# Two stages with no end inside: the delta heads, and the ssd part of a kernel on one core

## The reference

```python
qkv = jax.nn.silu(centred_dwconv(p[..., :DN_CONV_DIM], conv_w))
t_inv = triangular_solve(eye + a, eye)          # a: beta k k^T decay, strictly lower
v_new = u_i - w_i @ s
o = qd_i @ s + qk_i @ v_new                      # one chunk of the scan
s = s * gl_i + kd_i^T @ v_new
y = (rms_norm(o) * silu(z)) @ w_out
```

```python
xbc = jax.nn.silu(centred_depthwise_conv(xbc, conv_w, conv_b))   # x, B, C: 12 tiles
dt = jax.nn.softplus(dt_raw + dt_bias)
y = ssd_chunked(xs, dt, a, bm, cm)               # 16 heads, forward and backward
y = (y_f + y_b + xs * d_skip) * silu(z)          # z: 8 tiles
```

## Time and profile before

| what | us |
|---|---|
| median of three runs (2258.82 to 2260.98) | 2260.4 |
| the profiled execution | 2255.24 |
| its span, first to last instruction | 2253.5 |
| TensorE busy in it | 1979.7 (88%) |
| VectorE busy in it | 1049.9 (47%) |
| delta heads, from the first a_t transpose to the stage's end | 159.7 to 965.7 |
| ssd part, first product to the next part's first | 1293.9 to 1519.8 |

### The profile page before, as it was taken

The page is one execution under the profiler, slowest core; times in us unless marked ns, Lnnn a source line. Parts: engine busy times, 40 slices in busy tenths (PEclk is TensorE's granted clock), DMA queues, the critical chain, the costliest instruction groups (busy, mean ns, idle before and its releaser), DMA issues. The chain is left out here.

```text
span 2253.5 us, 40621 instructions
## 1 busy us (share of the span) xinstructions
PE 1979.7 (88%) x16700; PEld 1460.5 (65%) x16700; DVE 1049.9 (47%) x2118; ACT 587.4 (26%) x1255; POOL 76.1 (3%) x50
## 2 busy tenths in 40 slices
PE   5889898989898898789788787888899899989998
PEld 2356666666666566544376676666777598878887
DVE  3355756575656657511115417777544554221101
ACT  1033433434343434300103203223333322000000
POOL 0000101011010101000000000000000000000000
PEclk9899999999899999989899888998999999999999
DMA  8710101010101010022131232123000321434443
GB/s 333 298 52 7 57 2 59 1 58 1 59 1 58 8 51 1 2 112 75 42 113 38 78 140 89 65 89 132 31 30 30 140 76 44 165 132 156 157 170 131
DMA packets 52242, 184.77 MB, mean 82 GB/s; under 512 B 5856, under 2 KB 9312, under 8 KB 51552
## 3 DMA queue, kind: packets, MB, share of 16 engines
q1 hardware_dynamic: 52064, 182.23, 21.9%
HBM read 180.11 MB, written 2.10 MB: 81 GB/s over the span
## 5 line engine op out<-in xcount | busy, mean ns | idle before, releaser
L780 PE MATMUL banks<-u,w_ring 128*128 128x512 f32 x768 | 355.5, 600 | 6.5 <-PEq L195 6.5
L410 PE MATMUL banks<-u,w_ring 128*128 128x256 f32 x1088 | 248.8, 391 | 14.8 <-PEq L195 14.8
L410 PEld LDWEIGHTS banks<-u,w_ring 128*128 128x128 f32 x1088 | 212.4, 197 | 48.7 <-issue 18.9
L780 PEld LDWEIGHTS banks<-u,w_ring 128*128 128x128 f32 x768 | 141.1, 192 | 136.6 <-issue 133.4
L3146 PE MATMUL banks<-gated,w_ring 128*128 128x512 f32 (+1 forms) x384 | 140.7, 529 | 2.8 <-PEq L195 2.8
L386 PE MATMUL banks<-u,w_ring 128*128 128x256 f32 x480 | 118.8, 400 | 5.4 <-PEq L225 5.4
L441 PE MATMUL banks<-u,w_ring 128*128 128x256 f32 (+1 forms) x384 | 102.1, 430 | 20.2 <-PEq L195 20.2
L3146 PEld LDWEIGHTS banks<-gated,w_ring 128*128 128x128 f32 x384 | 73.9, 193 | 69.3 <-issue 66.0
L386 PEld LDWEIGHTS banks<-u,w_ring 128*128 128x128 f32 x480 | 94.0, 203 | 20.1 <-issue 7.6
L441 PEld LDWEIGHTS banks<-u,w_ring 128*128 128x128 f32 x384 | 75.4, 197 | 46.9 <-issue 38.0
L807 DVE SCALAR_TENSOR_TENSOR acc<-raw,hc,acc 128x512 f32<-128x512 f32 x128 | 96.2, 752 | 4.6
(11 more groups left out here) (496 smaller groups left out, 3227.1 us busy)
## 6 DMA issues: line engine op xcount, KB each, us to landing
w_ring<-in_w SPq DMA_DIRECT2D x321, 512.0 KB, 6.0
h<-in_h SPq DMA_DIRECT2D x2, 2048.0 KB, 9.6
const_base<-in_const SPq DMA_DIRECT2D x1, 1216.0 KB, 5.4
hold<-h SPq DMA_DIRECT2D x1, 1024.0 KB, 5.8
const_part<-in_const SPq DMA_DIRECT2D x1, 1024.0 KB, 4.8
h<-hold SPq DMA_DIRECT2D x1, 1024.0 KB, 9.2
out<-u SPq DMA_DIRECT2D x8, 128.0 KB, 1.9
const_part<-in_const SPq DMA_DIRECT2D x1, 640.0 KB, 4.4
```

The source lines that it names most:

```text
L410: last = nc.tensor.matmul(out, lhs[k], rhs[k], start=(k == 0), stop=(k == n - 1))
L780: mm = nc.tensor.matmul(self.places[m % len(self.places)][:, :], st.slot(m)[:, P * k:P * k + P], u[:, k, :], start=(k == 0), stop=(k == KT ...
```

## The change

Delta: the seven loop bodies and the last one become one stage, written out head after head, with every semaphore counted on from head to head (`COUNTS`, `due`, `up`). The loads go through `in_stage`. Waits that the stage's end gave for free are now written: `chained`, `dec_ready`, `o_out`, `gate_in`, `raw_out`, `kq_norm`, `silu` at the start of a head. `SCAN` goes down by one product in seven gaps, and the sixth tile (the second gate) of head n+1's front is projected in head n+1, four products ahead of the a_t transposes and four behind them. The output's transposes move before rows 2 and 3, and VectorE's output multiplications between its chains.

Ssd: all ten stages become one. The 36 projected tiles (12 of x, B, C, 8 of z, 16 of rwkv) run in one order on TensorE, in groups of six chunks; each x, B or C tile is taken out, convolved and turned behind its projection; the steps are made beside them; then 16 heads, with the decay rows two heads ahead. ScalarE makes the middle tap of the convolution with the bias; the silu is one VectorE operation. B and C are projected first, so the weights are laid out anew.

```diff
-    LAST, SCAN, REST = 1, ((0, 4, 4), (4, 4, 3), (4, 4, 3), (4, 4, 0)), 2
+    LAST, SCAN, REST = 1, ((0, 3, 3), (3, 3, 3), (3, 3, 3), (4, 3, 0)), 2
...
+        with stage(nc, names + front_names) as (s, block):
+            fronts = [Front(s, zs_of[(n + 1) % 2], hs_of[(n + 1) % 2], n) for n in range(QK_HEADS - 1)]
+            st.in_stage(QK_HEADS - 1, DN_GROUP, s["proj"], block)
...
+                if made:
+                    made.products(pe, KT // 2)
+                for c in (0, 2, 1, 3):
+                    if made:
+                        pe.wait_ge(s["chained"], made.up("chained", c + 1))
+                        pe.wait_ge(s["dec_ready"], made.up("dec_ready", 3 + c // 2 if c < 3 else 4))
+                        pe.wait_ge(s["o_out"], 2 * n)
+                    for t in range(TT):
+                        mm = nc.tensor.transpose(tile(bank[2 * (c % 2) + c // 2], t), tile(a_t[:, c, :], t), C("ident"))
+                    mm.then_inc(s["a_done"], 1)
+                if made:
+                    made.products(pe, KT // 2)
+                    pe.wait_ge(s["raw_out"], made.up("raw_out", 4))
+                    pe.wait_ge(s["kq_norm"], made.up("kq_norm", 2))
...
+                if more:
+                    front.scaled(dve, link)
+                    front.conv(dve, link, 3)
+                    front.chain(dve, link, 0)
+                    output(0)
+                    front.chain(dve, link, 1)
+                    output(1)
+                    front.chain(dve, link, 2)
+                    front.chain(dve, link, 3)
+                    front.silu(dve, link, 3)
```

The TensorE order of the ssd stage, and VectorE's heads:

```diff
+            extra.products(pe, 2 * KT)
+            step_rows()
+            extra.products(pe, 3 * KT)
+            step_sums()
+            for j in range(1, 8):
+                extra.products(pe, KT)
+                if j == 3:
+                    scores()
+                if j >= behind:
+                    turn(j - behind)
+            for j in range(8 - behind, 8):
+                extra.products(pe, KT)
+                turn(j)
+            rows(0)
+            rows(1)
+            for hh in range(SSM_HEADS):
+                if hh + 2 < SSM_HEADS:
+                    rows(hh + 2)
+                extra.products(pe, share(hh) // 2)
+                products(hh)
+                extra.products(pe, share(hh) - share(hh) // 2)
...
+            for hh in range(SSM_HEADS):
+                weights(hh)
+                if hh + 2 < SSM_HEADS:
+                    gaps(hh + 2)
+                if hh % 2 == 0 and hh:
+                    finished(hh // 2 - 1)
```

More of the change, by code:

```diff
@@ new lines, in scores, with turn @@
+            def scores():
+                pe.wait_ge(s["silu"], 4)
+                for g in range(2):
+                    for t in range(ST):
+                        mm = nc.tensor.matmul(bank[g][:, SEQ * t:SEQ * t + SEQ], p[:, 16 + g, P * t:P * t + P], p[:, 18 + g, :],
+                                              start=True, stop=True)
+                    mm.then_inc(s["cb_done"], 1)
+            def turn(j):
+                pe.wait_ge(s["silu"], 5 + j)
+                if j >= 2:
+                    pe.wait_ge(s["turned_out"], j - 1)
+                for t in range(ST):
+                    mm = nc.tensor.transpose(bank[2 + j % 2][:, P * t:P * t + P], p[:, 8 + j, P * t:P * t + P], C("ident"))
+                mm.then_inc(s["turned"], 1)
@@ new lines, in rows @@
+            def rows(hh):
+                if hh == 0:
+                    pe.wait_ge(s["steps"], 4)
+                    pe.wait_ge(s["cb_out"], 4)
+                if hh == 1:
+                    pe.wait_ge(s["turned_out"], 8)
+                if hh >= 2:
+                    pe.wait_ge(s["gaps"], 2 * hh - 2)
+                for d in range(2):
+                    for t in range(ST):
+                        mm = nc.tensor.matmul(bank[2 * (hh % 2) + d][:, P * t:P * t + P], col(hh, S_AC, d, t).to_broadcast([P, P]),
+                                              C("ident"), start=True, stop=True)
+                    mm.then_inc(s["rows"], 1)
@@ new lines, in products @@
+            def products(hh):
+                pe.wait_ge(s["weights"], hh + 1)
+                j, at = hh // 2, 64 * (hh % 2)
+                if j >= 2 and hh % 2 == 0:
+                    pe.wait_ge(s["done"], j - 1)
+                for t in range(ST):
+                    mm = nc.tensor.matmul(bank[4 + j % 2][at:at + 64, 0:SEQ], x_t[:, t, 64 * hh:64 * hh + 64],
+                                          m_t[:, hh % 2, SEQ * t:SEQ * t + SEQ], start=(t == 0), stop=(t == ST - 1))
+                mm.then_inc(s["ys"], 1)
@@ L1613, in _ @@
+            tanh(convs - 1)
+            for j in range(8 - behind, 8):
+                copy(convs + j - 8 + behind)
+                turned(j)
+            decays(0)
+            done, copied = behind * KT, behind
+            for hh in range(SSM_HEADS):
+                if hh + 1 < SSM_HEADS:
+                    decays(hh + 1)
+                done += share(hh)
+                while copied < done // KT:
+                    copy(convs + copied)
+                    copied += 1
         @block.vector
@@ new lines, in build @@
+            dt_rows = sb("dt_rows", [P, 2, 32], es)
+            work = [sb("ssd_" + n, [P] + d, es) for n, d in (
+                ("raw", [3, SEQ + 4]), ("acc", [3, SEQ]), ("th", [2, SEQ]), ("cb", [2, 2, 512]), ("x", [ST, D]), ("e", [3, 2, 512]),
+                ("m", [2, 512]), ("tz", [8, SEQ]), ("steps", [5, 32 * ST]), ("half", [72]))]
+            loads = start_loads(nc, [(w_dt[:, :, :].rearrange("p k c -> p (k c)"), a["w_dt"]),
+                                     (dt_rows[:, :, :].rearrange("p a c -> p (a c)"), a["rows"][:, 64:128].to_broadcast([P, 64])), pair], small)
@@ L2886, in build @@
+            ssd_heads(nc, st, bank, C2, cs, latent, w_dt, dt_rows[:, 0, :], dt_rows[:, 1, :], (small, loads), p, sc, cc("ssm_conv"),
+                      cc("ssm_conv_b"), cc("ssm_d"), work, ys, p_rw)
+            nc.sync.sem_clear(small)
         hg = top.enter_context(ExitStack())
```

1071 lines of the change are left out of this document (519 added, 552 removed).

## The result

The changed kernel takes 2163.4 us (median of four, 2161.9 to 2164.6) beside 2260.7: a ratio of 0.957, 95% interval 0.955 to 0.959, or 97 us less. The forecast was 2151, 110 less, with a range of 2136 to 2188. So the sign, the place and most of the size were right, and 12 us are missing (the forecast's own narrower range ended at 2163).

What follows compares the result with a forecast made beforehand. TensorE, busy for 88% of the span, was taken as the bound. Gains of 58 us (delta heads) and 51 us (ssd part) made 109 us, so 2151 us, own range 2136 to 2163, 2136 to 2188 with rivals.

Steps and rivals of the forecast that it cites:

- The scan gives the products back: Delta scans: with seven products fewer in the gaps, each head's scan gets 5.9 us shorter.
- Rival 1: Delta scans: ScalarE or VectorE sets the step, so nothing comes back; 41 us lost, 2192, chance 5%.
- The boundary: Between delta heads: VectorE's path takes 14.55 us against 15.91; with the earlier scan end, 7.25 us gained at each of seven.
- Rival 3: Delta boundaries: VectorE's tail stays in sight, 3 us each, 21 us in all, 2172; chance 8%.
- The back edges: Delta boundaries where the loop jumps back: idle beyond 5.88 us goes too, 8.5 us in all.
- The clock: Delta boundaries: TensorE's clock stays at its upper level, as the idle it follows is gone; transposes 2.6 us, not 5.3.
- the range's clock cases: Both parts: dense work without idle lowers TensorE's granted clock; under about 0.89 the whole gain goes, 2308 at 0.85; chance 2%.
- the sentence on the loads: Delta heads: a group's six loads start some 10 us into a head, 20 us before first use; no cost given.
- Rival 4: Delta heads: straight code starves the sequencers, one 4 us stall a head, 8 x 4 us, 2183; chance 5%.
- The ssd part: Ten ssd stages made one: TensorE's work and waits sum to 173.4 us against 225.9; 51 us taken as gain.
- The two table loads of ScalarE: Ssd steps: by the skill's price they hold ScalarE 5.3 us and cost 1 to 2 us; left out of the sum.
- Rival 2: Ssd heads: VectorE or the chain through it sets the pace, 7.8 us a head for 6.6; 20 us lost, 2171, 12%.

Runs made afterwards that it cites:

- e3_six: e1_late with the moved gate tile put back in the scan of the head before, one stage and new output places kept; ratio 0.9708.
- e1_late: The changed kernel with each delta group's six chunks loaded once the head's scan has begun, not beside the inverse; 2149.0 us, ratio 0.9505.
- e8_five_three: e1_late with the moved tile split five products ahead of the a_t transposes and three behind, not four and four; ratio 0.9523.
- e4_unrolled: The kernel before with its seven delta bodies written out, one stage each, without the hardware loop; ratio 0.9970.
- e6_gaps_twice: The changed kernel with each of the 64 subtractions of the ssd heads done twice on VectorE; ratio 0.9673.

## Why the prediction was right, and where it fell short

**The scan gives the products back: right.** Between e3_six and e1_late seven products move out of it and it shrinks from 60.28 to 54.67 us a head, 5.6 for a forecast of 5.9. Rival 1 falls.

**The boundary: right, and nearer to a tie than the sum said.** The five boundaries without a back edge took 10.9 to 12.3 us before, 11.8 in the mean, and take 13.3 now; the scan gave 8.67. That is 7.1 us a head for 7.25. I had VectorE's path to the second border (14.55 us) as the longer and TensorE's to the first at 9.5. VectorE's was right: 14.3, from 348.83 to 363.15 in the third head, and TensorE waits for its end there:

```profile
363.15 0.69 PE L1049 MATMUL banks<-acc,a_t 64*64 64x64 f32 x32 [0.35 <-DVE acc L1267]
```

TensorE's was wrong: it is busy for all of the 12.7 us to the first border but 0.4, since I left the turns of k and v, the output's transposes and the last decay rows out of the 9.5. So it nearly sets the boundary too, and e8_five_three, which moves one product, gains nothing. Rival 3 has 0.4 and 0.35 us, not 3.

**The back edges: right.** 8.5 us forecast, 8.6 measured as 2 x 4.3. Scans and boundaries together gave 60.2 - 2.3 = 57.9 us, the 58 of the forecast; what the stage lacks lies in the inverse (16.2 us).

**The clock: right at the boundary, wrong behind it.** The transposes run on the upper clock (2.4 GHz) as said. But of the range's clock cases I saw only dense work as a cause, and what came was idle from a new stall.

**Where 17 us went: the sentence on the loads.** Among the moves "with one answer" stood that the six loads now start some 10 us into a head, 20 us before their first use. True, and priced at nothing: I asked whether they come in time, not what they run beside. They run beside the inverse, 715 products in 22 us, and that costs 14.5 us by e1_late's time and 18.8 by its trace. From head to head it took 97.3 to 99.8 us for the forecast's 96; in e1_late 94.8 to 96.5. Rival 4 had the right organ, the instruction supply, at 32 us and 5%, with the wrong cause (straight code), for which e4_unrolled shows 3.3 us or nothing. The profile before could have told. In its second head the loads are issued from 263.1 on, and the timeline has, as the transfer ends:

```profile
273.85 0.45 PE L1015 MATMUL banks<-acc,a_t 64*64 64x64 f32 x11 [0.70 <-issue]
```

There the burst lay beside the slow transposes and met only the inverse's first levels. The last head, without loads, has no such wait.

**The ssd part: right.** 173.3 us for 173.4. The match to 0.1 us is luck in part: the waits, filling and end included, are 3.3 us for 4.7, and TensorE's work 170.0 for 168.7. The two table loads of ScalarE, for which the forecast named 1 to 2 us beside its sum, take 1.28 us each here, the next operation starts right behind each, and no wait of TensorE ends on them. Rival 2 falls for this kernel, and e6_gaps_twice shows that it was less than 2 us of VectorE a head away.

**The sum.** Delta 41.1 for 58, ssd part with the start of the next stage 53.5 for 51; 94.6 in all. The two profiled executions differ by 91.7, mostly because the stage starts 2.4 us later in the one of after; and the profiled one of before lies 5 us under its median, which makes the measured 97.

## What to carry to other kernels

A load has two questions, whether it comes in time and what it runs beside; a burst that fills the DMA engines belongs beside long instructions, not beside hundreds of short ones. An engine's tail at a stage's end is worth covering with the other engine's movable work even when the stage's end goes, for here the tile brought 46 us on top of the fused stage's 13. And where a segment that a change does not touch gets longer, cut both traces at the same lines before looking for a reason in the change.

## What the hardware showed that was not expected

TensorE's instruction supply is held up by other DMA traffic. With the DMA share at 1.0 for 8 us it stopped for 1.1 to 2.3 us in the midst of a group; moved into the scans, the same traffic left 1.3 us of such waits at the border products in the whole stage, where there had been 7.4. Each stall ends 1.2 to 1.6 us behind a 16 KB packet of the instruction queue. The Trainium skill, Runtime: NRT & Kernel Launch, section Instruction fetch mechanics, says that the sequential fetch stays hidden because an engine issues more slowly than the fetch fills. In this case that holds in the scans and without bulk traffic nearly everywhere, and fails beside a burst.

A stall of 1.4 to 2.9 us in the midst of dense work can halve TensorE's clock: thirteen such stalls in four traces were followed by 1.2 GHz for some 3 to 7 us. It need not: behind stalls of 0.8 to 1.6 us, and once behind 2.33, the clock stayed at 2.4 GHz. And a turn of the loop cost 4.3 us over the stage's end itself.
